# Working through the head pairs of both mixers two by two, with a second stick buffer

## What is computed

```python
# mixer of layer 0, per chunk of 64 queries
s = einsum(q_c, k_c) * scale + bias          # band of 576 keys, masked
y = einsum(softmax(s), v_c) @ w_o
# mixer of layer 1, per block of 128 queries
z = einsum(q_b, k_b) * scale
log_beta = where(causal, log_sigmoid(z), -inf); log_1m_beta = where(causal, log_sigmoid(-z), 0)
stick = reverse cumsum(log_1m_beta) - log_1m_beta
y = einsum(exp(log_beta + stick), v_b) @ w_o
# feed-forward
h = (silu(x @ w_gate) * (x @ w_up)) @ w_down
```

## Time and profile before

| what | value |
|---|---|
| time, median of 3 runs | 976.21 us (975.58 to 976.64) |
| the profiled execution | 976.81 us, of which the span on the core is 975.1 us |
| TensorE busy | 964.9 us, 99% |
| VectorE, ScalarE, GpSimd busy | 646.2, 488.5, 43.5 us |
| granted TensorE clock, mean | 0.998 |
| chain that ended last | TensorE 96% |

### The profile page before, as it was taken

The page is one execution under the profiler, slowest core; times in us unless marked ns, Lnnn a source line. Parts: engine busy times, 40 slices in busy tenths (PEclk is TensorE's granted clock), DMA queues, the critical chain, the costliest instruction groups (busy, mean ns, idle before and its releaser), DMA issues.

```text
span 975.1 us, 13384 instructions
## 1 busy us (share of the span) xinstructions
PE 964.9 (99%) x5202; PEld 814.9 (84%) x5202; DVE 646.2 (66%) x775; ACT 488.5 (50%) x611; POOL 43.5 (4%) x71
## 2 busy tenths in 40 slices
PE   8999999999999999999999999999999999999997
PEld 7888888888878888888888888888888788888886
DVE  6766673777567666664676666638777777666635
ACT  6555562366663555562245555443655445555530
POOL 0300000010101000000000000001112100000000
PEclk9999999999999999999999999999999999999999
DMA  9965566475453655557555555653744445555611
GB/s 341 309 201 202 175 212 225 167 234 184 157 171 99 238 184 183 201 179 256 173 174 188 199 176 196 243 188 131 256 148 151 152 141 205 179 200 181 227 76 43
DMA packets 53612, 183.91 MB, mean 189 GB/s; under 512 B 5920, under 2 KB 9664, under 8 KB 53568
## 3 DMA queue, kind: packets, MB, share of 16 engines
q1 hardware_dynamic: 50864, 175.00, 52.7%
q0 software_dynamic: 2560, 8.18, 2.6%
q10 hardware_dynamic: 144, 0.13, 0.1%
HBM read 182.21 MB, written 1.07 MB: 188 GB/s over the span
## 4 chain that ended last, share of the span: by engine, by line
PE 96%; DVE 1%; DMA 1%; issue 1%; SPq 0%; ACT 0%; POOLq 0%; POOL 0%; DVEq 0%
PE psum L405 30%; PE psum L409 15%; PE psum L354 12%; PE psum L356 12%; PE psum L355 12%; PE psum L557 6%; PE psum L560 3%; PE psum L597 1%; PE psum L607 1%; PE psum L342 1%; DMA raw<-in_units 1%; PE psum L619 1%; DVE w_lo L895 0%; SPq L297 0%; PE psum L620 0%
## 5 line engine op out<-in xcount | busy, mean ns | idle before, releaser
L886 DVE TENSOR_TENSOR w_lo<-raw,w_hi 128x2048 fp32r<-128x2048 f32 x160 | 364.6, 2290 | 192.1 <-ACT w_hi L684 191.7
L405 PE MATMUL psum<-xT,w_hi 128*128 128x512 f32 x1280 | 402.4, 396 | 0.6 <-DVE w_lo L895 0.6
L684 ACT ACTIVATE w_hi<-raw 128x2048 fp32r<-128x2048 f32 x160 | 303.2, 1906 | 90.0 <-PE psum L356 89.9
L409 PEld LDWEIGHTS psum<-xT,w_lo 128*128 128x128 f32 x1280 | 240.5, 188 | 56.8
L409 PE MATMUL psum<-xT,w_lo 128*128 128x256 f32 x1280 | 251.5, 278 | 0.0
L405 PEld LDWEIGHTS psum<-xT,w_hi 128*128 128x128 f32 x1280 | 195.1, 189 | 1.3 <-DVE w_lo L895 1.1
L354 PE MATMUL psum<-w_hi,hT_hi 128*128 128x512 f32 (+1 forms) x422 | 164.3, 389 | 0.0
L355 PE MATMUL psum<-w_lo,hT_hi 128*128 128x512 f32 (+1 forms) x422 | 163.0, 386 | 0.0
L356 PE MATMUL psum<-w_hi,hT_lo 128*128 128x512 f32 (+1 forms) x422 | 163.0, 386 | 0.0
L727 ACT ACTIVATE hT_hi<-hiddenT 128x256 f32 (+1 forms) x82 | 34.2, 418 | 200.0 <-DVE hiddenT L915 200.0
L356 PEld LDWEIGHTS psum<-w_hi,hT_lo 128*128 128x128 f32 x422 | 79.3, 188 | 16.2
(11 more groups left out here) (87 smaller groups left out, 660.1 us busy)
## 6 DMA issues: line engine op xcount, KB each, us to landing
raw<-in_units SPq DMA_DIRECT2D x324, 512.0 KB, 4.7
gain<-in_ln_g POOLq DMA_DIRECT2D x6, 512.0 KB, 3.9
shift<-in_ln_b POOLq DMA_DIRECT2D x6, 512.0 KB, 5.0
first<-in_first SPq DMA_DIRECT2D x7, 384.0 KB, 8.0
x<-in_x SPq DMA_DIRECT2D x1, 1024.0 KB, 15.1
rel<-bias_by_distance POOLq DMA_DIRECT2D x8, 128.0 KB, 4.5
rel<-bias_by_distance POOLq DMA_DIRECT2D x8, 96.0 KB, 4.3
out<-x SPq DMA_DIRECT2D x2, 256.0 KB, 2.1
```

Of the source, the lines that this page charges most:

```text
L405: pe.matmul(TILE[j][:, which, :], as_gu(w_hi[s])[:, k, at:at + P], xT[:, kk, :, :], start=kk == 0, stop=False)
L409: last = pe.matmul(TILE[j][:, which, 0:SEQ], as_gu(w_lo[s])[:, k, at:at + P], xT[:, kk, 0, :], start=False, stop=kk == KD - 1)
L684: act.activation(w_hi[slot][:], raw[raw_slot][:], ACT.Copy).then_inc(hi_done, 1)
L886: dve.tensor_tensor(w_lo[slot][:], raw[raw_slot][:], w_hi[slot][:], ALU.subtract).then_inc(lo_done, 1)
```

## The change

Both mixers go through the pairs two by two. TensorE does two `qk_block`s with other weight work between them, then two `turn_probs` in a row, other weight work, two `head_out`s in a row and two `scores` in a row. For this `probsT` gets a second buffer (over `gate_act` and `hidden`, which the mixer doesn't use), `stick` a second one over the bias tables `rel`, and the head output a second half of PSUM bank 4; the two outputs of a couple are taken out by one instruction each on ScalarE and VectorE. The order of the weight units, their slots and the orders of ScalarE and VectorE are new. The last unit's split in a mixer (`n0 + 17`, the next feed-forward block's second unit) now stands behind the first half of the layer norm (`norm(t, 0)`) on VectorE, and behind the last head output on ScalarE. The number of matmuls stays; ScalarE and VectorE each have six head-output instructions fewer (three of double size in place of six, per mixer).

```diff
-MIX_ORDER = [("v", 0, 0), ("v", 0, 1), ("qk", 0), ("v", 1, 0), ("qk", 1), ("v", 1, 1), ("qk", 2), ("qk", 3),
-             ("qk", 4), ("qk", 5), ("o", 0), ("qk", 6), ("o", 1), ("qk", 7), ("o", 2), ("o", 3)]
+MIX_ORDERS = [
+    [("v", 0, 0), ("v", 0, 1), ("qk", 0), ("v", 1, 0), ("qk", 1), ("qk", 2), ("v", 1, 1), ("qk", 3),
+     ("qk", 4), ("qk", 5), ("qk", 6), ("o", 0), ("qk", 7), ("o", 1), ("o", 2), ("o", 3)]] * DEPTH
...
+BEFORE_PAIRS = [[("v", 0, (0, 1))], [("v", 0, (2, 3))]]
+BETWEEN_QK = [[("v", 0, (4, 5, 6, 7))], [("v", 1, (2, 3, 4))], [("o", 0, 0, 0)]]
+BEHIND_TURN = [[("v", 1, (0, 1))], [("v", 1, (5, 6, 7))], [("o", 1, 0, 0)]]
+LAST_PAIRS = [[("o", 0, 0, 1), ("o", 0, 1, 0), ("o", 1, 0, 1), ("o", 2, 0, 0)], [("o", 2, 0, 1)], [("o", 0, 1, 1)]]
...
-MIX_SLOTS = [0, 1, 4, 2, 3, 0, 4, 1, 3, 4, 1, 3, 2, 0, 3, 4]
+DOUBLE = (0, 1)
+MIX_SLOTS = [[0, 1, 4, 2, 3, 0, 3, 4, 1, 0, 4, 1, 0, 2, 3, 4]] * DEPTH
...
+        gate_at = nc.sbuf_base
...
+        probsT = [probsT, nc.alloc_sbuf_tensor_at("probsT1", [P, 2, KEYS], F32, offset=gate_at)]
...
+        rel_at = nc.sbuf_base
...
+        stick = [stick, nc.alloc_sbuf_tensor_at("stick1", [P, 2, KEYS], F32, offset=rel_at)]
...
-        HEADOUT = psum[:, 4, 0:SEQ]
+        HEADOUTS = psum[:, 4, :].rearrange("p (k n) -> p k n", k=2)
+        HEADOUT = [psum[:, 4, p * SEQ:(p + 1) * SEQ] for p in range(2)]
...
             def head_out(m, pp):
                 pe.wait_ge(probsT_done, m * PAIRS + pp + 1)
-                if m * PAIRS + pp > 0:
+                if m * PAIRS + pp > 0 and not (m in DOUBLE and pp in (1, 3, 5)):
                     pe.wait_ge(headout_lo, m * PAIRS + pp)
                 if pp == GROUPS:
                     pe.wait_ge(v_copied, m * 4 + 4)
                 for h in range(2):
-                    acc = HEADOUT[h * HD:(h + 1) * HD, :]
+                    acc = HEADOUT[pp % 2][h * HD:(h + 1) * HD, :]
                     cols = slice((2 * pp + h) * HD, (2 * pp + h + 1) * HD)
-                    pe.matmul(acc, v[:, 0, cols], probsT[:, h, 0:2 * P], start=True, stop=False)
-                    last = pe.matmul(acc[:, P:2 * P], v[:, 1, cols], probsT[:, h, 2 * P:3 * P],
+                    pe.matmul(acc, v[:, 0, cols], probsT[pp % 2][:, h, 0:2 * P], start=True, stop=False)
+                    last = pe.matmul(acc[:, P:2 * P], v[:, 1, cols], probsT[pp % 2][:, h, 2 * P:3 * P],
                                      start=False, stop=True)
...
+            def pairs_by_two(m):
+                for pp in range(2):
+                    qk_block(m, pp)
+                    for todo in BEFORE_PAIRS[pp]:
+                        fill(m, todo)
+                for pp in range(2):
+                    scores(m, pp)
+                for c in range(PAIRS // 2 - 1):
+                    qk_block(m, 2 * c + 2)
+                    for todo in BETWEEN_QK[c]:
+                        fill(m, todo)
+                    qk_block(m, 2 * c + 3)
+                    for pp in (2 * c, 2 * c + 1):
+                        turn_probs(m, pp)
+                    for todo in BEHIND_TURN[c]:
+                        fill(m, todo)
+                    for pp in (2 * c, 2 * c + 1):
+                        head_out(m, pp)
+                    for pp in (2 * c + 2, 2 * c + 3):
+                        scores(m, pp)
+                for todo in LAST_PAIRS[0]:
+                    fill(m, todo)
+                turn_probs(m, PAIRS - 2)
+                for todo in LAST_PAIRS[1]:
+                    fill(m, todo)
+                turn_probs(m, PAIRS - 1)
+                head_out(m, PAIRS - 2)
+                for todo in LAST_PAIRS[2]:
+                    fill(m, todo)
+                head_out(m, PAIRS - 1)
+
+            def mixer_matmul(m, t, finish):
+                v_block(m, 0, 0, range(KD), t, TURN_BETWEEN)
+                transpose_x(t, 1, (2,))
+                v_block(m, 0, 1, range(KD), t)
+                (pairs_by_two if m in DOUBLE else pairs_by_one)(m)
...
             def sigmoids(m, pp):
                 act.wait_ge(scores_done, m * PAIRS + pp + 1)
-                if pp >= 1:
-                    act.wait_ge(probs_ready, m * PAIRS + pp)
-                act.activation(stick[:], SCORES[pp % 2], ACT.Sigmoid, scale=-SCALE).then_inc(sigmoid_done, 1)
+                if pp >= 2:
+                    act.wait_ge(probs_ready, m * PAIRS + pp - 1)
+                act.activation(stick[pp % 2][:], SCORES[pp % 2], ACT.Sigmoid, scale=-SCALE).then_inc(sigmoid_done, 1)
                 if pp >= 2:
                     act.wait_ge(probsT_psum, m * PAIRS + pp - 1)
                 act.activation(probs[pp % 2][:], SCORES[pp % 2], ACT.Sigmoid, scale=SCALE).then_inc(sigmoid_done, 1)
 
             def probsT_copy(m, pp):
                 act.wait_ge(probsT_psum, m * PAIRS + pp + 1)
-                if m * PAIRS + pp > 0:
-                    act.wait_ge(headout_done, m * PAIRS + pp)
-                act.activation(probsT[:], SCORES[pp % 2], ACT.Copy).then_inc(probsT_done, 1)
+                if m * PAIRS + pp > 1:
+                    act.wait_ge(headout_done, m * PAIRS + pp - 1)
+                act.activation(probsT[pp % 2][:], SCORES[pp % 2], ACT.Copy).then_inc(probsT_done, 1)
+
+            def headout_hi_two(m, pp):
+                act.wait_ge(headout_done, m * PAIRS + pp + 2)
+                act.activation(hT_hi[:, pp:pp + 2, :], HEADOUTS, ACT.Copy).then_inc(headout_hi, 2)
...
+            def weights_by_two(m, n0):
+                weights = exps if m % 2 == 0 else sigmoids
+                hi_unit(n0 + 4)
+                hi_unit(n0 + 5)
+                qk_copy(m, 0)
+                qk_copy(m, 1)
+                hi_unit(n0 + 6)
+                hi_unit(n0 + 7)
+                weights(m, 0)
+                weights(m, 1)
+                qk_copy(m, 2)
+                hi_unit(n0 + 8)
+                copy_v(m, 1, 0)
+                hi_unit(n0 + 9)
+                qk_copy(m, 3)
+                probsT_copy(m, 0)
+                probsT_copy(m, 1)
+                hi_unit(n0 + 10)
+                headout_hi_two(m, 0)
+                weights(m, 2)
+                weights(m, 3)
...
+                weights(m, 6)
+                weights(m, 7)
+                hi_unit(n0 + 16)
+                probsT_copy(m, 6)
+                probsT_copy(m, 7)
+                headout_hi_part(m, 6)
+                headout_hi_part(m, 7)
+                hi_unit(n0 + 17)
...
-            def sticks(m, pp):
+            def sticks(m, pp, between=None):
 
                 dve.wait_ge(masked_done, 2 * pp + 1)
+                st = stick[pp % 2]
                 for h in range(2):
-                    dve.tensor_tensor_scan(stick[:, h, ::-1], stick[:, h, ::-1], restart[:, ::-1], 1.0,
+                    dve.tensor_tensor_scan(st[:, h, ::-1], st[:, h, ::-1], restart[:, ::-1], 1.0,
                                            ALU.mult, ALU.max).then_inc(stick_done, 1)
+                    if h == 0 and between:
+                        between()
 
             def break_sticks(m, pp):
 
                 dve.wait_ge(masked_done, 2 * pp + 2)
                 dve.wait_ge(stick_done, 2 * pp + 2)
                 dve.tensor_tensor(probs[pp % 2][:, :, 0:KEYS - 1], probs[pp % 2][:, :, 0:KEYS - 1],
-                                  stick[:, :, 1:KEYS], ALU.mult).then_inc(probs_ready, 1)
+                                  stick[pp % 2][:, :, 1:KEYS], ALU.mult).then_inc(probs_ready, 1)
...
+            def pairs_by_two(m, n0):
+                if m % 2 == 0:
+                    first, second = soften, normalise
+                else:
+                    first, second = sticks, break_sticks
+                qk_add(m, 0)
+                lo_unit(n0 + 5)
+                qk_add(m, 1)
+                lo_unit(n0 + 6)
+                for c in range(PAIRS // 2):
+                    a, b = 2 * c, 2 * c + 1
+                    if 0 < c < PAIRS // 2 - 1:
+                        headout_lo_two(m, a - 2)
+                    first(m, a)
+                    if c == PAIRS // 2 - 1:
+                        headout_lo_two(m, a - 2)
+                    if m % 2 == 0:
+                        first(m, b)
+                    else:
+                        second(m, a)
+                    if c == 0:
+                        lo_unit(n0 + 7)
+                    if m % 2 == 0:
+                        if c == 0:
+                            qk_add(m, 2)
+                        second(m, a)
+                        second(m, b)
+                    else:
+                        first(m, b, (lambda: qk_add(m, a + 2)) if b + 1 < PAIRS else None)
+                        second(m, b)
+                    if c == 0:
+                        lo_unit(n0 + 8)
+                        lo_unit(n0 + 9)
+                        qk_add(m, 3)
+                        lo_unit(n0 + 10)
+                    if c == 1:
+                        if m % 2 == 0:
+                            qk_add(m, 4)
```

(72 more changed lines are left out.)

31 lines of the change are left out of this document (12 added, 19 removed).

## The result

The changed kernel takes 978.55 us (median of 15 runs, 977.22 to 979.95) against 976.28 us (15 runs, 975.58 to 977.11) for the kernel before: ratio 1.0023, 95% interval 1.0017 to 1.0029. That is 2.3 us, a little over the 0.2% that I had called the least that can be told. The profiled execution took 978.33 us with a span of 976.6 us, 1.5 us more than before. The forecast was 976.7 (974.8 to 978.6).

A forecast was written before the change was run, and what follows sets the result against it. TensorE, 99% busy at full clock, was taken as the bound. The terms -3.4 + 0.8 + 2.4 + 0.2 + 0.6 gave +0.6 us (+0.5 before rounding): 976.7 against 976.21, range 974.8 to 978.6 leaving out 2 in 10.

The forecast's parts named there:

- TensorE's order (-3.4): TensorE, both mixers: runs of one kind side by side save edges, 1.7 us per mixer, 3.4 for both.
- The rival that each run drains towards the next of its kind: TensorE: a run drains even towards the next of its own kind; +2 us, 978.7; chance 0.07.
- `qk_block` 1 and 7 (+0.8): Both mixers: these blocks wait for the copy and sum of the block before, 0.20 us each, 0.8 in all.
- The second mixer's first couple (+2.4): TensorE waits 2.4 us ahead of `qk_block(3)` for VectorE's `qk_add(2)`; 1.0 of it without disturbance by selects.
- the lock: Second mixer's first couple: GpSimd's selects and VectorE's scans, `break_sticks` and split exclude each other; three selects cost 1.35 us.
- The rival without a late sum: Second mixer's first couple isn't late, TensorE keeps the 3.4 us and pays only small waits; 974.4 us; chance 0.12.
- The one with losses in every couple: Second mixer: GpSimd's selects and VectorE's work stop each other in every couple; +1.8 us, 978.5; chance 0.16.
- The last couple (+0.2): Second mixer: TensorE waits 0.2 us (0 to 0.9) at `turn_probs(7)` for both pairs' scans and selects.
- The ends (+0.6): End of each mixer: unit 17's split makes the `xT` sums and second-half norm 0.3 us later, twice: 0.6.

The follow-up runs named there:

- e7: First mixer by two, second as before, with nine weight matmuls ahead of `qk_block(1)` and three behind, for six and six; ratio 0.9996 to the kernel before.
- e4: Changed kernel without GpSimd's select of `probs` for pairs 0 and 1 of the second mixer (timing only); ratio 1.0011 to the kernel before.
- e6: Changed kernel with second-mixer moves: `qk_add(2)` before `break_sticks(0)`, first sigmoids before a weight copy, `headout_lo` of pairs 4 and 5 before pair 6's scans; 975.34 against 975.95 us.
- e9: Changed kernel with the second mixer's `qk_add(2)` behind all of pair 1 on VectorE; ratio 1.0058 to the kernel before.
- e2: Only the second mixer goes by two, the first as in the kernel before; 979.36 us, ratio 1.0031 to the kernel before.
- e3: Changed kernel with the second mixer's `qk_add(2)` ahead of pair 0's `break_sticks` and pair 1's first scan on VectorE; ratio 1.0001 to the kernel before.
- e8: Second mixer alone by two, run once more for its trace; the traced execution took 980.7 us at a mean clock of 0.996.
- e5: The changed kernel itself, measured again beside other kernels; 978.07 us against 975.95 for the kernel before, ratio 1.0025.

## Why the prediction was right, and where it was off

The time came inside the range, but at its upper end, 1.9 us above the forecast; the measured interval of the loss, 0.17 to 0.29%, lies across the 0.2% that I had set between the same and slower, and I had given 0.72 to the same and 0.17 to slower. The mechanism was the one forecast; 1.2 us of the miss are in the terms of the sum, the rest is outside of it.

**TensorE's order (-3.4).** Right in kind, too large in size. Going from one run to the next of its own kind costs nothing for scores (1.51 for 1.50) and transposes, and 0.04 for head outputs (1.50 for 1.46). A whole cycle of two pairs takes 19.80 against 20.20 for two old ones with the same fill, so it saves 0.40 where I had 0.47. Three cycles and two mixers make 0.4 us. The rival that each run drains towards the next of its kind is out.

**`qk_block` 1 and 7 (+0.8).** Mis-sized: 0.38 each, not 0.20, four times over +0.7. In the changed kernel six weight matmuls and the wait take 1.67 (1.37 undisturbed):

```profile
209.91 0.40 PE L367 MATMUL psum<-w_hi,xT 128*128 128x512 f32 x1
...
211.05 0.39 PE L369 MATMUL psum<-w_hi,xT 128*128 128x512 f32 x1
211.58 0.70 PE L570 MATMUL psum<-xT,w_hi 128*128 128x512 f32 x2
```

The block behind takes 5.65 instead of 5.56. The wait was 0.30 for 0.20, and the block behind it takes 0.08 more, which the sum had nowhere. e7, where `qk_block(1)` has a longer cover, shows both gone there.

**The second mixer's first couple (+2.4).** Measured 2.19 in W12 and 0.10 in the block behind it, 2.29. That it came out right was in part luck, two errors that cancel: the lock took 1.03 rather than 1.35, as it never reached the split, and the chain without it was 1.2 late rather than 1.0. The lock works both ways here: the selects grew from 0.64 to 1.10 and 1.28. That agrees with the rule of the Trainium skill, page SBUF — State Buffer, section Who interferes with whom, that the two exclude each other; that the loser stands for a whole instruction no row here shows, as a select of 0.67 cost the scans 0.41 (e4). The 1.1 us that GpSimd lost cost nothing by themselves, as nobody waited for the last select. The rival without a late sum is out. The one with losses in every couple had the lock right and the wait wrong: the first scans of pairs 2, 4 and 6 take 2.62 to 2.65 as well, but TensorE's weight loads stood ahead of L570 in only five places in the whole kernel, `qk_block` 1 and 7 of both mixers and this one (us in total, times, longest):

```profile
PEld psum L570 <- issue: 4.5, 5, 2.4
```

**The last couple (+0.2).** Measured +0.44, of which 0.32 have a reason that I had not seen: the two-wide `headout_lo` stands behind pair 6's scans, which the lock stretches, and the output projection on TensorE needs it.

```profile
761.86 2.65 DVE L1211 TENSOR_TENSOR_SCAN stick<-stick,restart 128x384 f32<-128x384 f32 x2 [3.18 <-POOL stick L1403]
764.43 0.66 DVE L1232 TENSOR_TENSOR hT_lo<-psum,hT_hi 128x512 fp32r<-128x512 f32 x1
```

```profile
764.78 0.39 PE L369 MATMUL psum<-w_hi,hT_lo 128*128 128x512 f32 x1
765.24 0.47 PE L367 MATMUL psum<-w_hi,hT_hi 128*128 128x512 f32 x1
```

The 24 weight matmuls took 5.92, in the first mixer 5.60. With `headout_lo` moved (e6) they take 5.60 in the second one too. The other 0.12 are at `turn_probs(7)` and the weights ahead of it (0.80 and 1.53 against 0.75 and 1.46), the wait that I had priced at 0.2. Here I had looked only at what `turn_probs(7)` waits for, not at what the moved head output feeds.

**The ends (+0.6).** Measured +0.61 in both mixers together. The wait that this term leans on isn't in the earlier trace rows, to which I had pointed; it is another line of the same list of the kernel before:

```profile
PEld psum L342 <- DVE x L967: 2.8, 7, 0.4
```

So the terms make, against the forecast: +0.4 + 0.7 - 0.1 + 0.2 = +1.2 where the traces show 1.75 - 0.5 = 1.25.

**What the sum did not hold.** The median lies 0.5 us further up than the stretches say (2.27 for 1.75). The falls of the clock are there in part of the executions, and I had taken TensorE's full clock in the earlier trace rows as given for the changed kernel and priced the wait at its own length. Five of 15 runs at 1.55 us would add 0.5 us to the mean (an estimate from the section on the clock); the means differ by 2.07. That the ten other runs lie 1.6 us over the kernel before, and that e9, whose trace contains the fall, lies only 0.2 over its stretches, fits this. The falls aren't all of the spread, though. The traced execution of e2 took 979.07 us without one, and it reached its first `qk_block` at 204.67 us, late in the range of 203.8 to 204.7. e3 lies 0.5 over its stretches without such runs, within its interval of 0.9 either way; so half a microsecond alone would prove nothing. Open stays what decides in which executions the clock falls behind a wait of 2.0 us, and how much of e2's 1.3 us over its stretches is more than three runs of six at 0.996.

## What to carry to other kernels

Putting runs of one kind side by side on a full TensorE saves its edges, here 0.4 us per two pairs; the price is that everything one couple needs from the other engines now falls due at once, so write down for each moved sum and copy who waits for it, not only for the last one. One stop of 2 us ate nearly all of six such savings (2.29 of 2.4). Such a stop can be dearer than it is long: in some executions the clock fell behind it, for 1.55 us more.

## What the runs showed of the hardware

- The granted clock fell to 1.2 GHz for 3.4 us, from 0.4 us after TensorE had restarted, behind one stop of 2.0 us in an otherwise full stream (e8's trace). Behind the same stop it did not fall in the traces of after, e2 and e5. Behind a stop of 4.0 us it fell in e9's trace, from 1.2 us after the restart. Either time it cost 1.55 to 1.57 us (blocks of 7.21 and 7.23 for 5.66).
- The block behind a wait takes 0.08 to 0.10 us more than undisturbed (5.65 and 5.66 for 5.56), however long the wait: behind 2.0 us in after as behind the 0.03 us that is left in e6 (5.65).
- A pair of scans on VectorE took 1.79 alone, 2.20 with one select of GpSimd beside it, 2.64 with three; the selects took up to 1.28 instead of 0.64.
